# One pattern of zero products for every FFN, GLU and Fourier mixer, and for the longer streams of panels in the attention and selective mixers

## The reference

```python
def swiglu(h, w_gate_up, w_down):
    gate, up = jnp.split(h @ w_gate_up, 2, axis=-1)
    return (jax.nn.silu(gate) * up) @ w_down        # 1024 -> 2 x 2816 -> 1024

def fourier_mixer(h, w_out):                        # real part of a 2D FFT per group of 128
    ...
    return f.reshape(b, s, d).astype(h.dtype) @ w_out

def s5_mixer(...):
    ...
    val, gate = jnp.split(g @ w_glu, 2, axis=-1)    # the GLU, 1024 -> 2 x 1024
    return val * jax.nn.sigmoid(gate)
```

## Time and profile before

| | |
|---|---|
| runs | 2603.05, 2591.95, 2603.62 us; median 2603.05 |
| profiled execution | 2603.65 us |
| its span, first to last instruction | 2601.8 us |
| TensorE | products 2495.0 us, weight loads 2436.6 us of it |
| VectorE, ScalarE, GpSimd | 1778.3, 1259.3, 216.0 us |
| read from memory | 426.45 MB, 164 GB/s over the span |

### The profile page before, as it was taken

The page is one execution under the profiler, slowest core; times in us unless marked ns, Lnnn a source line. Parts: engine busy times, 40 slices in busy tenths (PEclk is TensorE's granted clock), DMA queues, the critical chain, the costliest instruction groups (busy, mean ns, idle before and its releaser), DMA issues.

```text
span 2601.8 us, 54597 instructions
## 1 busy us (share of the span) xinstructions
PE 2495.0 (96%) x23182; PEld 2436.6 (94%) x23182; DVE 1778.3 (68%) x2300; ACT 1259.3 (48%) x1508; POOL 216.0 (8%) x246
## 2 busy tenths in 40 slices
PE   7999759999999899999999999999999999999998
PEld 7999759999999889989999999999999998999998
DVE  5988966556555666657666669876657667986665
ACT  5434445334566653344344346565335335665433
POOL 5000050003000100000000000500000000320000
PEclk9999879999999999999999999999999999999999
DMA  5553014555677735535545544434555554443553
GB/s 214 183 189 125 19 67 176 180 191 169 187 174 182 174 117 193 192 133 189 192 172 206 193 171 154 147 130 165 191 183 185 191 193 147 152 147 146 179 194 127
DMA packets 65839, 430.76 MB, mean 166 GB/s; under 512 B 8288, under 2 KB 11360, under 8 KB 15904
## 3 DMA queue, kind: packets, MB, share of 16 engines
q1 hardware_dynamic: 58864, 410.30, 44.1%
q0 software_dynamic: 6000, 17.46, 4.5%
q10 hardware_dynamic: 832, 0.92, 0.1%
HBM read 426.45 MB, written 1.15 MB: 164 GB/s over the span
## 4 chain that ended last, share of the span: by engine, by line
PE 88%; DVE 7%; ACT 3%; issue 1%; DMA 0%; DVEq 0%; ACTq 0%
PE psum L2020 26%; PE psum L2022 26%; PE psum L2021 26%; DVE w_lo L1332 1%; ACT w_hi L847 1%; PE psum L2070 1%; PE psum L2235 1%; PE psum L2141 1%; PE psum L2384 1%; DVE h L1351 1%; PE psum L2372 1%; DVE h_lo L1340 1%; PE psum L2362 1%; PE psum L2124 0%; PE psum L2328 0%
## 5 line engine op out<-in xcount | busy, mean ns | idle before, releaser
L2020 PE MATMUL psum<-h_hi,w_hi 128*128 128x256 f32 x4320 | 1215.1, 281 | 16.4 <-DVE h_lo L1376 9.6
L2021 PE MATMUL psum<-h_lo,w_hi 128*128 128x256 f32 x4320 | 1205.0, 279 | 0.0
L2022 PE MATMUL psum<-h_hi,w_lo 128*128 128x256 f32 x4320 | 1204.6, 279 | 0.0
L847 ACT ACTIVATE w_hi<-raw 128x2048 fp32r<-128x2048 f32 x387 | 741.2, 1916 | 857.1 <-PE psum L2022 857.1
L1332 DVE TENSOR_TENSOR w_lo<-raw,w_hi 128x2048 fp32r<-128x2048 f32 x387 | 886.8, 2292 | 386.9 <-ACT w_hi L847 386.5
L2020 PEld LDWEIGHTS psum<-h_hi,w_hi 128*128 128x128 f32 x4320 | 816.1, 189 | 26.0 <-issue 20.8
L2021 PEld LDWEIGHTS psum<-h_lo,w_hi 128*128 128x128 f32 x4320 | 815.8, 189 | 0.6 <-issue 0.5
L2022 PEld LDWEIGHTS psum<-h_hi,w_lo 128*128 128x128 f32 x4320 | 815.5, 189 | 0.0
L2020 PE MATMUL psum<-act_hi,w_hi 128*128 128x256 f32 x1536 | 427.3, 278 | 0.7 <-DVE act_lo L1895 0.7
L2021 PE MATMUL psum<-act_lo,w_hi 128*128 128x256 f32 x1536 | 426.1, 277 | 0.0
L2022 PE MATMUL psum<-act_hi,w_lo 128*128 128x256 f32 x1536 | 426.0, 277 | 0.0
(11 more groups left out here) (342 smaller groups left out, 2386.5 us busy)
## 6 DMA issues: line engine op xcount, KB each, us to landing
raw<-in_panels SPq DMA_DIRECT2D x387, 1024.0 KB, 4.8
arena<-bias_by_distance POOLq DMA_DIRECT2D x32, 384.0 KB, 6.2
x<-in_x SPq DMA_DIRECT2D x1, 1024.0 KB, 5.6
arena<-in_s_cbd POOLq DMA_DIRECT2D x4, 256.0 KB, 3.0
arena<-in_s_b SPq DMA_DIRECT2D x1, 1024.0 KB, 15.2
arena<-in_s_c SPq DMA_DIRECT2D x1, 1024.0 KB, 17.2
hidden<-in_s_cbd POOLq DMA_DIRECT2D x4, 256.0 KB, 2.8
arena<-arena POOLq DMA_DIRECT2D x32, 32.0 KB, 1.9
```

The source lines that it names most:

```text
L847: a.activation(w_hi[:, s, :], raw[:, s, :], ACT.Copy).then_inc(hi_ready, 1)
L2020: t.matmul(o, w[0], xin[0], start=start, stop=False, skip_group_check=True)
L2021: t.matmul(o, w[0], xin[1], start=False, stop=False, skip_group_check=True)
L2022: return t.matmul(o, w[1], xin[0], start=False, stop=stop, skip_group_check=True)
```

## The change

The FFNs' lists go. One dictionary `PACE` takes their place: a wide zero product at (0, 0) and (0, 4) and a narrow one (2 columns) at (1, 4). It is what FFN 7 has had. All eight FFNs, both Fourier mixers and the GLU use it in panel 1. `lead` keeps two forms, `wide` true or false. New places: in the dilated attention a wide product at (0, 0) and a narrow one at (1, 0) of the first panel of blocks 1 to 3; in each selective mixer `PACE` in panel 1, the wide and narrow pair at (0, 0) and (1, 0) of panel XBC + 1, and in output panel OUT_ATT + 1 a wide one ahead of tile 0 and a narrow one ahead of tile 4, 24 products later.

```diff
-        FFN_LEADS = [{(1, 0): 1}, {(1, 0): 2}, {(0, 4): 0}, {(0, 2): 0, (1, 2): 0}, {(0, 0): 3, (1, 0): 0},
-                     {(0, 0): 2}, {(0, 0): 3, (1, 0): 1}, {(0, 0): 3, (0, 4): 3, (1, 4): 0}]
+        PACE = {(0, 0): True, (0, 4): True, (1, 4): False}
...
-            def lead(o, start=True, form=0):
...
-                z = zeros[:, :].bitcast(F32)
-                if form == 0:
+            def lead(o, start, wide):
...
+                if wide:
+                    t.matmul(o[:, 0:E], zeros[:, :], zeros[:, 0:E], start=start, stop=True, skip_group_check=True)
+                else:
+                    z = zeros[:, :].bitcast(F32)
                     t.matmul(o[:, 0:2], z, z[:, 0:2], start=start, stop=True, skip_group_check=True)
...
-                project(n0 + 1, 1, led=FFN_LEADS[f])
+                project(n0 + 1, 1, led=PACE)
...
-                    project(st["n0"] + p, p, ..., led={(0, 0): 0} if p == 1 else None)
+                    project(st["n0"] + p, p, ..., led=PACE if p == 1 else None)
...
                 def panel(p):
                     hb, i, _ = da_panel(p)
+
+                    led = {(0, 0): True, (1, 0): False} if p and i == 0 else None
...
-                        project(n0 + p, 0, o=o, parts=None if p else (h_lo_ready, 4 * st["hs"]))
+                        project(n0 + p, 0, o=o, parts=None if p else (h_lo_ready, 4 * st["hs"]), led=led)
...
-                        project(n0 + p, p, parts=(h_lo_ready, 4 * st["hs"]) if p == 0 else None)
+                        project(n0 + p, p, parts=(h_lo_ready, 4 * st["hs"]) if p == 0 else None,
+                                led=PACE if p == 1 else {(0, 0): True, (1, 0): False} if p == XBC + 1 else None)
...
                     t.wait_ge(lo_ready, n0 + p + 1)
                     for c in tiles:
+                        if p == OUT_ATT + 1 and c in (0, 4):
+                            lead(bank[k], False, c == 0)
```

More of the change, by code:

```diff
@@ L2022, in mm3 @@
                 return t.matmul(o, w[1], xin[0], start=False, stop=stop, skip_group_check=True)
-            def lead(o, start=True, form=0):
-                z = zeros[:, :].bitcast(F32)
-                if form == 0:
-                    t.matmul(o[:, 0:2], z, z[:, 0:2], start=start, stop=True, skip_group_check=True)
[L2030 to L2036, removed]
+            def lead(o, start, wide):
[3 more added lines that the diff above has]
+                    z = zeros[:, :].bitcast(F32)
+                    t.matmul(o[:, 0:2], z, z[:, 0:2], start=start, stop=True, skip_group_check=True)
             def weights(n, lo, width=P):
@@ L2145, in fourier @@
                 for p in range(4):
-                    project(st["n0"] + p, p, parts=None if p else (dft_lo_ready, f * KT // 2), frees=(p == 3), led={(0, 0): 0} if p == 1 else None)
+                    project(st["n0"] + p, p, parts=None if p else (dft_lo_ready, f * KT // 2), frees=(p == 3), led=PACE if p == 1 else None)
             def s5_mixer(st):
@@ L2285, in s5_mixer @@
                         t.wait_ge(x_ready, st["xr"] + p // 2 - 1)
-                    project(st["n0"] + p, p, parts=None if p else (s5_g_lo_ready, 0), frees=(p == 7), led={(0, 0): 0} if p == 1 else None)
+                    project(st["n0"] + p, p, parts=None if p else (s5_g_lo_ready, 0), frees=(p == 7), led=PACE if p == 1 else None)
             def project_tokens(n, o, tokens):
```

## The result

| | median us | range, executions |
|---|---|---|
| before | 2603.02 | 2584.37 to 2617.39, 16 |
| after | 2587.84 | 2581.18 to 2590.77, 16 |

The account below looks back on a forecast made before the run. The prediction took TensorE, 96% busy, and its spacing of 128x256 products as the bound. FFNs -20.4, Fourier and GLU +1.1, dilated attention 0.0 and mixers -0.9 summed to -20.2 us: 2583 us, range 2577 to 2593.

Parts of the forecast that it names:

- The pace mechanism: FFN loops: a narrow product turns TensorE's stream from 117.8 to 113.3 ns per product; three slow loops gain 20.5 us.
- The price of the three zero products: `PACE` on TensorE: two wide products at 0.11 us and a narrow one at 0.22, together 0.44 us.
- The gain of FFN 0: FFN 0's faster stream passes whole through the S5 stage behind it; were it hidden there, 6.5 us would be lost.
- the danger at 90 us: FFN 0: VectorE's `w_lo` might come late for a faster TensorE; its 1.3 us margin shrinks to some 0.4.
- a stream begins slow after small products: TensorE's product streams start at the slow pace after small products, until a narrow product can turn them fast.
- the 0.4 us each of the sum: Two Fourier mixers and the GLU: `PACE` costs 0.22 us more and the pace starts 36 products later, +1.1 us together.
- the bounds: Dilated attention: three panels cost 0.33 us each and regain 0.32, so nothing; a miss costs at most +0.33 per panel.
- -20.4 + 1.1 + 0: Everything but the selective mixers: FFNs -20.4 us, Fourier and GLU +1.1, dilated attention 0.0.
- the mixers': -0.9: Two selective mixers: zero products and faster streams net -0.45 us each; with a miss at each place, +1.1 per mixer.
- 3 us either way for the clock: Whole kernel: half-clock stretches after TensorE's waits, about 11 us in all, may get shorter or longer by 3 us.
- The zero products only add: Rival: the pace belongs to stage and addresses, so the lists only cost, +3.8 us, or 2607 us; chance 0.08.
- A narrow product that can't turn the stream: Rival: behind two wide products the narrow one misses everywhere, fast loops turn slow, 2643 us; chance 0.04.

Follow-up runs that it names:

- after again: The changed kernel once more, with no edit: 2588.55 us, ratio 0.9949 to the kernel before.
- FFNs only: Changed kernel with `PACE` only in the FFNs, Fourier and GLU as before the change, no zero products in dilated attention and selective mixers: 2580.23 us.
- without the mixers: Changed kernel without any zero product in the two selective mixers: 2579.17 us, ratio 0.9902 to the kernel before.
- output pair: Changed kernel keeping, in the selective mixers, only the wide and narrow products of panel OUT_ATT + 1: 2581.63 us, ratio 0.9907 to the kernel before.
- warm: Changed kernel with only the OUT_ATT + 1 products in the mixers, plus 40 zero products of 256 columns ahead of each mixer's first panel: 2577.39 us.
- before again: The kernel before the change once more, one execution for another profile: 2608.3 us.
- none: Changed kernel without any of the zero products of `lead`: 2633.02 us, ratio 1.0153 to the kernel before.
- inside 1: Changed kernel with the narrow product of `PACE` moved behind the first product of the group at (1, 4): 2629.29 us, ratio 1.0132 to the kernel before.

## Why the prediction was right, and what it mis-sized

**The pace mechanism held.** All eight loops have 1326 products where five had. Inside FFN 5, from its sum of squares to that of FFN 6, the time fell from 189.59 to 182.62 us: 7.0, against a forecast of 1548 x 4.45 ns + 0.38 = 7.3. The price of the three zero products fits. The gain of FFN 0 came through S5, and the danger at 90 us did not come: the waits show none there. Over six profiles with `PACE` ahead of the group (after, after again, FFNs only, without the mixers, output pair, warm) 47 of 48 loops were fast. The miss was FFN 2 in *only the output pair*; its stream was fast before the wide product of (0, 4), which left it slow and in the wrong pattern. The prediction's "a stream begins slow after small products" does not hold always: that stream, FFN 0's in *before again* and the GLU's in *none* began fast.

**Fourier, GLU and dilated attention.** The changed kernel's Fourier mixers and GLU were all hit, as forecast; whether they cost the 0.4 us each of the sum is below what these runs can tell. One place of three in the dilated attention was missed, at 0.65 us, and it was the same one in each of the seven profiles that had the wide and narrow pair there. It was within the bounds.

**The sum without the selective mixers.** The forecast for everything but them was -20.4 + 1.1 + 0 = -19.3. Without their zero products the kernel is 2602.61 - 2579.17 = 23.4 us faster between the medians, but the interval of the ratio (0.9866 to 0.9939) spans 16 to 35 us, so that the sum was too small is not shown. The sum started from one profile with five fast loops. The kernel before has other sets in other executions: its profile was at 2603.65 with five, the second at 2608.3 with four, and its runs reach from 2574 to 2624. The two profiles of the first comparison can be set side by side. Outside the two stretches that hold a mixer, each with the loop ahead of it, the time fell by 20.6 us, against a forecast of 19.6. One part of it was not in the sum: from FFN 0's sum of squares to FFN 1's the time fell by 9.6 us, where the terms give 6.1, and of the two kernels only the one before has a stretch of 6.8 us at clock 0.50 there, at 263.6 us.

**The term that was mis-sized is the mixers': -0.9 forecast, about +9 measured** (+9.4 between the medians, +6.7 between the profiles). The prediction's bound was +1.1 for each. The zero products did what was said of them: 276 ns from panel 1 on. But with them `w_lo`, which follows TensorE's panels through ScalarE, comes some tenths later against GpSimd, and a `w_lo` that had been 0.03 to 0.09 us ahead of a GpSimd add came to be behind it. Then a second price follows from the first: a longer wait on TensorE, and half clock behind it. The prediction allowed 3 us either way for the clock and nothing for the collision. The changed kernel came out at -23.4 + 9.4 = -14.0 in that comparison and at -15.2 in the first one. That 2587.84 lies in the range is in part luck: the range had room for one missed loop, no loop was missed in the profile, and the mixers took up that room.

**Not settled.** Why the slow stream carries its long distance at one place or another, and why a narrow product acts on it as it does: the rule above is counted, not explained. How the 9 us divide between the collision and the clock is open, but the profiles lean to the clock. The eight stretches of loop and mixer with a collision, each slow loop taken off at 6.6 us, fall in order of the half clock behind it: with 6.8 us at 0.50 they took 433.0 to 434.2 us (four), with 3.4 us 430.1 to 431.5 (three), and with none 429.1, in the second mixer of *inside 1* (435.7 - 6.6), about the 428.9 without a collision. So in that one case the collision, without half clock behind it, was hardly paid for. The dilated attention's first place was not mended.

**The rivals.** "The zero products only add" fell with *none*: the rival expected 2580 us, and it took 2633.02, 28 over the median of the kernel before. "A narrow product that can't turn the stream" is real, but at another place in the group of three; between groups, behind two wide products, it almost never came. A single miss happened in 1 loop of 48.

## What to carry to other kernels

Where identical instructions show two durations that hold for a whole stream, count instructions in equal windows first, and then look at what stands just ahead of the stream: here 4 ns a product, decided by one instruction of 0.22 us, were worth 45 us between all loops slow and all fast. Put such a product where the stream is long (an FFN's 1500 products) and leave it out where the stream is short and closely timed work of other engines follows, as at the start of the mixers, where it could give back 0.5 us and cost 3 to 5. And when a change delays one engine by tenths of a microsecond, look in the old trace for pairs that start within a tenth of each other on VectorE and GpSimd: their order is part of the schedule.

## What the runs showed that I had not expected

- A stream of 128x256 products at full clock has two steady paces, 113.3 and 117.8 ns, and the slow one carries a pattern of three with one distance about 1 ns longer. One narrow product changes the pace, depending on its place in that pattern: 136 of 136 turned fast at two of the places, 0 of 17 at the third, and 3 of 3 fast streams turned slow.
- `w_lo` and GpSimd's add of 32x512 exclude each other; the loser ends 1.0 us late (`w_lo`) or 2.1 us late (the add), decided by 0.03 to 0.17 us.
- Filling a wait of 4.8 us with 40 zero products kept the granted clock at 1.00 where it had been 0.50 for 6.8 us.
